# Selection half rounds moved from the recurrent mixer's inverse levels into the attention units

## The reference

```python
h = rms_norm(x, norm_g[l]); proj = h @ w_in[l]
o_a = dsa_mixer(...)              # A: top-k keys by an indexer score, then softmax attention
o_b = gated_deltanet_mixer(...)   # B: recurrence over chunks
o_c = nsa_mixer(...)              # C: compressed, selected and window attention
merged = g_a * (y_a @ wb[:A]) + g_b * (y_b @ wb[A:A+B]) + g_c * (y_c @ wb[A+B:])
x = x + merged @ w_out[l]

# inside A, for a block of 128 queries:
score = sum_h w_h * relu(q_idx_h . k_idx)        # masked to the past
_, sel = lax.top_k(score, 128)                   # 128 of up to 512 keys for each query
# inside B, for a chunk and a head:
t_inv = triangular_solve(eye + a_mat, eye)       # a 128 x 128 inverse here, two halves of 64
u = t_inv @ (v * beta) ; v_new = u - (t_inv @ w) @ state ; o = q @ state + attn @ v_new
```

## Time and profile before

| | |
|---|---|
| median of 3 runs | 604.04 us (603.85 to 605.86) |
| the profiled execution | 606.39 us, of which the span is 604.5 us |
| PE busy | 548.3 us (91%), 4087 matmuls |
| DVE busy | 388.2 us (64%), 920 instructions |
| ACT busy | 322.2 us (53%) |
| POOL busy | 221.1 us (37%) |
| granted PE clock | 0.989 of full speed on average |

### The profile page before, as it was taken

One profiled execution on the slowest core, in us unless ns is written; L12 is line 12 of the kernel. 1 busy time (PEld: TensorE's weight loads), 2 busy tenths in 40 slices (PEclk: granted clock), 3 DMA queues, 4 the chain that ended last, 5 costly groups with the idle time before them and its releaser, 6 DMA issues.

```text
span 604.5 us, 10710 instructions
## 1 busy us (share of the span) xinstructions
PE 548.3 (91%) x4087; PEld 306.8 (51%) x4087; DVE 388.2 (64%) x920; ACT 322.2 (53%) x573; POOL 221.1 (37%) x164
## 2 busy tenths in 40 slices
PE   2999999999999848999899998989898998899997
PEld 1544556543457423566475665545555564333443
DVE  6521397765498696777867778578896664576311
ACT  4555745356567844542624523876767675345320
POOL 0154453522046742242730712432323463234420
PEclk9999999999999997999999999999999998999999
DMA  9346865644024420220220201211221212252411
GB/s 318 109 122 155 149 107 156 206 127 117 26 54 123 121 89 2 70 72 1 75 66 3 74 32 35 72 36 36 70 71 36 71 36 69 71 210 70 140 52 53
DMA packets 31173, 52.93 MB, mean 88 GB/s; under 512 B 2743, under 2 KB 13329, under 8 KB 31121
## 3 DMA queue, kind: packets, MB, share of 16 engines
q1 hardware_dynamic: 30825, 51.68, 29.9%
q10 hardware_dynamic: 296, 0.55, 0.5%
HBM read 49.80 MB, written 2.42 MB: 86 GB/s over the span
## 4 chain that ended last, share of the span: by engine, by line
PE 66%; DVE 19%; ACT 7%; issue 5%; SPq 2%; DMA 1%; POOL 0%; DVEq 0%; ACTq 0%; PEldq 0%; POOLq 0%
PE bank L1683 13%; PE bank L1685 11%; PE bank L1684 11%; PE bank L1979 5%; PE bank L1981 5%; PE bank L1889 5%; PE bank L1983 5%; PE bank L1881 3%; PE bank L1719 3%; ACT stage L740 2%; PE bank L1825 2%; DVE bank L1258 1%; DVE early L1292 1%; DVE small L1289 1%; ACT late L962 1%
## 5 line engine op out<-in xcount | busy, mean ns | idle before, releaser
L528 POOL TENSOR_TENSOR w_lo<-stage,w_hi 128x1024 f16<-128x1024 f32 (+4 forms) x76 | 149.5, 1971 | 226.3 <-ACT w_hi L748 226.2
L748 ACT ACTIVATE w_hi<-stage 128x1024 f16<-128x1024 f32 (+4 forms) x76 | 74.5, 981 | 14.2 <-PE bank L1685 9.2
L1979 PE MATMUL bank<-hT_hi,w_hi 128*128 128x512 f16 x192 | 73.0, 380 | 1.7 <-PE bank L1983 0.9
L740 ACT ACTIVATE stage<-stage,small 128x512 f32<-128x512 f32 (+4 forms) x120 | 73.6, 663 | 0.5 <-DMA stage<-in_w_in 0.5
L1981 PE MATMUL bank<-hT_lo,w_hi 128*128 128x512 f16 x192 | 72.9, 380 | 0.3
L1983 PE MATMUL bank<-hT_hi,w_lo 128*128 128x512 f16 x192 | 72.8, 379 | 0.3 <-PE bank L1685 0.2
L1683 PE MATMUL bank<-w_hi,hT_hi 128*128 128x260 f16 (+4 forms) x192 | 60.9, 317 | 3.3 <-DVE hT_lo L1066 1.4
L1685 PE MATMUL bank<-w_hi,hT_lo 128*128 128x260 f16 (+4 forms) x192 | 60.8, 316 | 0.0
L1684 PE MATMUL bank<-w_lo,hT_hi 128*128 128x260 f16 (+4 forms) x192 | 60.7, 316 | 0.0
L1683 PE MATMUL bank<-hT_hi,w_hi 128*128 128x512 f16 (+1 forms) x128 | 48.1, 376 | 2.5 <-ACT work L731 1.5
L1685 PE MATMUL bank<-hT_hi,w_lo 128*128 128x512 f16 (+1 forms) x128 | 47.8, 374 | 0.0
(11 more groups left out here) (331 smaller groups left out, 1139.4 us busy)
## 6 DMA issues: line engine op xcount, KB each, us to landing
stage<-in_w_in SPq DMA_DIRECT2D x40, 512.0 KB, 3.7
stage<-in_c_phi_w SPq DMA_DIRECT2D x8, 512.0 KB, 4.0
stage<-in_w_branch SPq DMA_DIRECT2D x8, 512.0 KB, 3.9
stage<-in_w_out SPq DMA_DIRECT2D x8, 512.0 KB, 4.3
stage<-in_w_in SPq DMA_DIRECT2D x8, 260.0 KB, 2.8
strips<-rel_rows SPq DMA_DIRECT2D x8, 256.0 KB, 7.1
late<-in_x SPq DMA_DIRECT2D x1, 2048.0 KB, 9.1
out_x<-late SPq DMA_DIRECT2D x8, 256.0 KB, 2.0
```

What stands on the lines that cost most here:

```text
L528: gp.tensor_tensor(piece_view(w_lo[:, k % PAIRS, :], c), piece_view(stage[:, piece_at[c, j] % STAGES, :], c), piece_view(w_hi[:, k % PAIRS ...
L740: ins = nc.scalar.activation(full[:, r, :], full[:, r, :], ACT.Copy, scale=g_w[:, 2 * j + r:2 * j + r + 1])
L748: nc.scalar.activation(piece_view(w_hi[:, k % PAIRS, :], c), full, ACT.Copy).then_inc(hi_ready, 1)
L1979: mm(G.bank(g)[:, :], w[0], h[0], start=k == 0, stop=False)
```

## The change

Between the steps of an inverse level DVE did two half rounds after the z copy and one more at the end of the level; now it does one after the z copy and none at the end. In attention, units 1 to 27 asked for one half round each; now units 1 to 31 ask for two. Nothing else is touched.

```diff
@@ -1488,7 +1488,6 @@
                 def between_steps(l, late_in_level=False):
 
                     if l < 3 or next(extras, "end") == "end":
-                        rounds(1)
                         if not late_in_level:
                             rounds(1)
 
@@ -1600,8 +1599,8 @@
                 if u == 0:
                     for _ in norm:
                         pass
-                elif u < 28:
-                    rounds(1)
+                elif u < 32:
+                    rounds(2)
                 for f in Y_EARLY.get(u, ()):
                     y_lo(f)
```

## The result

The changed kernel takes 620.65 us (median of four runs, 620.28 to 620.99), the kernel before 604.45 us beside it (603.85 to 605.86): 1.027 times as long, 95% interval 1.0244 to 1.0295. The forecast was 614.6 us in a range of 609.5 to 621, slower with 0.95.

The account below looks back on a forecast made before the run. The prediction took TensorE to bound the recurrence and DVE attention units 16 to 23. Attention's loss of 13.0 us less the recurrence's gain of 2.4, added to 604.04, gave 614.6 us, range 609.5 to 621.

Parts of the forecast that it names:

- The bound: TensorE idles only 7.5 us in the recurrence; in attention units 16 to 23 DVE, 93% busy, sets the pace.
- How much is moved: From recurrence to attention: 36 half rounds leave the one for the other, 24.2 us of DVE time.
- The recurrence: Recurrence stage: TensorE waits for DVE behind only a few half rounds, so removing them gains 2.4 us.
- The wait in level 2: Recurrence, chunks 1 and 2: TensorE's wait falls from 0.54 to near 0.24 us, together 0.6 us gained.
- chunk 3: Last chunk of the recurrence: TensorE's waits of 0.40, 0.90 and 0.37 us shrink, gaining 1.4 us.
- Units 16 to 31: Late attention: with DVE 93% busy, the groups of four units last 3.2, 3.2, 3.7 and 1.4 us longer.
- Units 1 to 15: Early attention, taken as one group at 93% DVE: 8.5 us of added work makes it 1.5 us longer.
- The sum: Whole kernel: 13.0 us lost less 2.4 gained is 10.6 us slower, 614.6 us from a median of 604.04.
- the clock rival: Attention units 16 to 27: new waits drop TensorE's clock, 0.8 us more per unit, about 620 us; chance 17%.
- In series: Attention: engine latencies add to DVE's queue, so all 24.2 us are lost, 626 us; chance 6%.
- Attention absorbs more: Attention: DVE packs to 100%, losing only 6.7 to 9 us, 608.5 to 610.5 us in all; chance 13%.
- Faster: Recurrence regains all 7.5 us and attention loses only 6.7: 0.8 us faster, 603.2 us; faster or equal 4%.

Follow-up runs that it names:

- rec_only: Kernel before with only the recurrence part of the change, the 36 half rounds left out, so the selection is incomplete: 600.98 us, ratio 0.9923.
- att_only: Changed kernel's attention, with repeats of the last operation replacing the half rounds removed from the recurrence: 623.19 us, ratio 1.0291 against the kernel before.
- chunk3_only: Kernel before with only the 11 half rounds of the recurrence's chunk 3 moved, to attention units 1 to 11: 607.75 us, ratio 1.0037.
- split_pair: Changed kernel with one half round of each attention pair put ahead of the low half of the probabilities: 624.44 us, ratio 1.0306 against the kernel before.
- lo_in_four: Changed kernel with GpSimd's low parts of the weights made in four instructions each from attention on: 616.44 us, ratio 1.019 against the kernel before.
- slots: Kernel before with nine half rounds brought forward from attention to the ends of the recurrence's chunks: 604.23 us, ratio 0.9992.
- best1: Kernel before with early_decay and slots together, and eight half rounds among the last convolutions done later: 604.22 us, ratio 0.998.
- lo_all: Kernel before with every low part that GpSimd makes done in four instructions of a quarter each: 602.49 us, ratio 0.9953.
- early_decay: Kernel before with chunk 0's decayed products and the compressed keys ahead of ten half rounds and two convolutions in DVE's list: 603.27 us, ratio 0.997.

## Why the prediction was right, and where it was short

- **The bound** (TensorE hardly waits in the recurrence, DVE is the bound in units 16 to 23): right. `rec_only` and `att_only` show both signs apart.
- **How much is moved** (24.2 us): right. DVE's busy time fell by 23.1 us in the recurrence (107.36 to 84.26) and rose by 26.8 in attention (61.20 to 87.97), of which 4.5 are GpSimd's hold, so 22.3 are half rounds.
- **The recurrence** (gain 2.4): mis-sized, 3.6. `att_only` gained 2.7 of it with narrower half rounds alone, which the forecast did not part from fewer. The wait in level 2 fell to 0.25 as said. The short term is chunk 3: forecast 1.4, and `chunk3_only`, which changes only it, measures 2.15. I had taken the 0.90 us wait down to 0.24; it went to 0.15, and other small waits went with it. The rest, 1.45, stands against 1.0.
- **Units 16 to 31** (sum 11.5 of the 13.0): the mechanism held, DVE at 94 to 95% where I took 93; the size is in part luck. By the group starts 3.8, 3.7, 3.2 and 2.0 us against 3.2, 3.2, 3.7 and 1.4. The sum is 12.7, and 2.9 of it is the held instructions (0.74, 0.72, 1.76, less 0.35): without them 9.8 against 11.5, so a term that was left out filled one that was too large. Nor was the wait about 1 us in each unit, as I said; units 16 to 27 have three of 1.7 to 2.6 us and nine of 0.3 to 0.5.
- **Units 1 to 15** (1.5 longer): the step that failed, with 4.6 us. Of the 3.1 above the forecast, 1.6 are the hold at 405.58 and 1.5 the pooling of 15 units: their 28.4 us of 38.2 looked like room for all, but units 1 to 3 can't use theirs (DVE 76% even after), and units 4 to 15 were full with two half rounds each (90, 92 and 93%). Four windows apart, as for the later units, would have shown it: my rule on the first four of the earlier trace rows, with the same added work, gives 0, 0.4, 1.4 and 1.1 us, 2.9 in all, and 4.6 less the hold is 3.0. `chunk3_only` confirms it, though not for units 1 to 3, which lost 1.5 us where the rule in four windows gives nothing. It stayed below the 5 us at which I would have called the step wrong, but only just.
- **What was left out**: GpSimd's hold, 4.5 us net.
- **The sum.** By the profiles 14.0 us against 10.6: -1.2 in the recurrence, +4.3 in attention, +0.3 ahead of both, 3.4 in all. The other 2.6 of the 6.0 us between 614.6 and 620.65 are my base and the draw of runs: I took 2.3 us off a profile as if they were noise, and most of that is the clock behind the gap at 505 us, which fell in this profile and falls in only some executions. That 620.65 still lies in the range is luck: its upper end, 621, was the price of the clock rival, which did not happen.
- **The rivals.** In series: refuted by `split_pair`'s unchanged groups and by attention's 17.3 us, where it needed 24.2. Attention absorbs more: refuted, 17.3 us. The clock: refuted for this kernel's profile, whose clock is 1.00 in every group up to unit 31, with 18 waits that sum to 19.1 us. (Its mean clock over the whole span was 0.986 there and 0.983 to 0.989 in the timed runs, so in these it is not shown.) So the rule of the Trainium skill that the prediction weighed ("TensorE: Matmul & The Clock Gate", "A second HAM failure mode: psum-queue depth-cycling", that frequent micro-idles can be enough) is not borne out by this trace: the many waits of 0.3 to 0.7 us changed nothing. In its sisters the clock fell in attention in or just behind single waits of 1.4 us (`lo_in_four`), 1.8 (`split_pair`), 2.2 (`slots`) and 2.3 to 3.0, but stayed behind 3.1 in `best1` and behind four of 2.3 to 2.6 in this kernel. My price for it, 0.8 us for each unit, was wrong as well: 0 in units 24 to 27 of `att_only`, where DVE's list is longer.
- **Faster**: refuted; 3.6 us is the whole gain with all 36 moved.

## What to carry to other kernels

Before moving filler work to another stage, split that stage until each window has one kind of unit, and add up the receiving engine's list for one unit; an average share of idle time over 15 units hid 1.5 us here and, with what units 1 to 3 lost, 4 in `chunk3_only`. Then look for instructions of that engine that take many times their usual duration: each is a meeting with another engine, and a denser list brings more of them. Cutting the other engine's long instruction into pieces went with 0.5% here with no other change (`lo_all`), more than any rearrangement of half rounds that keeps the selection whole and these instructions uncut (at most 0.3%, `early_decay`), though part of it came by way of the clock.

## What the runs showed of the hardware

- **DVE waits for GpSimd's whole instruction.** A 128x4 multiply took 1.78 us for 0.17, a 128x16 copy 2.18 us, a 128x256 copy 2.23 for 0.29, each ending with GpSimd's 128x1024 subtraction of 2.13 us. The Trainium skill, "SBUF — State Buffer", section "SBUF: two separate sides", calls the pair's shared port an exclusive lock that is held for the whole of an instruction; the traces agree, with ends 0.02 us apart. What I had not expected is that instructions so small pay in full, and that in four pieces the wait per meeting in attention falls to 0.16 to 0.52 us.
- **It depends on the instruction, not on its size.** The 128x4 reciprocal at 440.90 kept its 0.18 us beside the same subtraction that held the 128x4 multiply behind it. In these traces the multiplies and subtractions of two SBUF operands, the copies and the scalar operations from SBUF to SBUF were held (those on 128x1 not, nor some that began at almost the same moment as the subtraction). Instructions with a PSUM operand, such as the logits (0.55 us at 425.95) and `probs_lo` (0.42 at 426.62, beside a subtraction that runs from 425.80 to 428.02), were not.
- **MAX8 and MATCH_REPLACE8 don't pay.** The row at 440.19 lies whole within the subtraction from 439.87 to 442.00 and keeps its 0.68 us. Over the fourteen profiles 115 MAX8 and 113 MATCH_REPLACE8 started beside a subtraction that had 0.3 us or more to run, and none took 0.02 us more than elsewhere. The half rounds themselves are immune; what they do is to shift the instructions between them into GpSimd's way.
- **The same gap may or may not cost the clock.** A wait of 2.47 us in after left it at 1.00, one of 2.48 us in `att_only` brought 0.50 (1.2 GHz), and the windows of before and `rec_only` show the same for the gap at the end of attention. What decides between them no run here shows. At the end of attention it makes 1.7 us of the scatter of this kernel, as much as several of the edits tried.
